# Root-mean-square means as two fp32r products, a reordered start-up, and reordered entries of two layers, in a fp32 network on one core

## What is computed

```python
def rmsnorm(x, g):
    xf = x.astype(jnp.float32)
    y = xf * lax.rsqrt(jnp.mean(xf * xf, axis=-1, keepdims=True) + EPS)
    return (y * g.astype(jnp.float32)).astype(x.dtype)

def swiglu(x, w_gate, w_up, w_down):
    return (jax.nn.silu(x @ w_gate) * (x @ w_up)) @ w_down

    h = x
    for l in range(DEPTH):                      # first_block
        h = h + 0.5 * swiglu(rmsnorm(h, ffn1_norm[l]), ffn1_w_gate[l], ffn1_w_up[l], ffn1_w_down[l])
        u = rmsnorm(h, mix_norm[l])
        z = u @ w_in[l]
        ...
        h = h + merged @ w_out[l]
        h = h + 0.5 * swiglu(rmsnorm(h, ffn2_norm[l]), ffn2_w_gate[l], ffn2_w_up[l], ffn2_w_down[l])
    return rmsnorm(h, final_norm)

        h = rms_norm(x, even_norm_g[i])         # second_block, layer 0
        proj = h @ even_w_in[i]
        ...
        x = x + jnp.concatenate([o_a, o_b], axis=-1) @ even_w_out[i]

        h = rms_norm(x, odd_norm_g[i])          # second_block, layer 1
        proj = h @ odd_w_in[i]
        q, k, v, z, r = jnp.split(
            proj, [GLA_KEY, 2 * GLA_KEY, 2 * GLA_KEY + GLA_VAL,
                   2 * GLA_KEY + 2 * GLA_VAL], axis=-1)
        log_a = jax.nn.log_sigmoid((r @ gla_w_gate[i] + gla_b_gate[i]).astype(jnp.float32)) / GLA_TAU
        ...
        x = x + (o * jax.nn.silu(z)) @ odd_w_out[i]
```

## Time and profile before

| | |
|---|---|
| time, median of 3 runs | 1449.96 us (1448.96 to 1450.06) |
| the profiled execution's own time | 1450.0 us |
| its span in the trace | 1448.1 us |
| granted TensorE clock | 1.00 of full speed |
| TensorE busy | 1441.7 us, 12390 matmul records |
| VectorE, ScalarE, GpSimd busy | 1051.4, 782.1, 99.2 us |
| moved by DMA | 261.37 MB, mean 180 GB/s |

### The profile page before, as it was taken

The page is one execution under the profiler, slowest core; times in us unless marked ns, Lnnn a source line. Parts: engine busy times, 40 slices in busy tenths (PEclk is TensorE's granted clock), DMA queues, the critical chain, the costliest instruction groups (busy, mean ns, idle before and its releaser), DMA issues.

```text
span 1448.1 us, 28457 instructions
## 1 busy us (share of the span) xinstructions
PE 1441.7 (100%) x12390; PEld 1392.2 (96%) x12390; DVE 1051.4 (73%) x1434; ACT 782.1 (54%) x1014; POOL 99.2 (7%) x77
## 2 busy tenths in 40 slices
PE   9999999999999999999999999999999999999999
PEld 8999998999999999999999899999999999989978
DVE  6766676797876655766558689888787799666844
ACT  6544556575554444544436566455645655775753
POOL 0000010210000000000001020000000037300000
PEclk9999999999999999999999999999999999999999
DMA  8655546444555655556554544466655454435531
GB/s 324 226 186 201 177 155 211 154 147 150 200 196 193 204 180 199 196 184 203 184 201 139 201 146 161 161 218 222 203 185 196 146 202 151 143 107 176 193 139 59
DMA packets 38844, 261.37 MB, mean 180 GB/s; under 512 B 4672, under 2 KB 5184, under 8 KB 9152
## 3 DMA queue, kind: packets, MB, share of 16 engines
q1 hardware_dynamic: 38576, 259.54, 52.2%
q10 hardware_dynamic: 144, 0.00, 0.0%
HBM read 258.48 MB, written 1.05 MB: 179 GB/s over the span
## 4 chain that ended last, share of the span: by engine, by line
PE 98%; DVE 1%; DMA 1%; ACT 0%; SPq 0%; issue 0%
PE ps L257 30%; PE ps L259 30%; PE ps L258 30%; PE ps L1549 1%; PE ps L1564 1%; DMA w_raw<-in_weights 1%; PE ps L1540 0%; PE ps L1522 0%; PE ps L2432 0%; DVE w_low L231 0%; PE ps L2866 0%; PE ps L2881 0%; PE ps L2453 0%; PE ps L2878 0%; PE ps L2465 0%; PE ps L1566 0%
## 5 line engine op out<-in xcount | busy, mean ns | idle before, releaser
L224 ACT ACTIVATE w_high<-w_raw 128x2048 fp32r<-128x2048 f32 (+1 forms) x243 | 457.3, 1883 | 478.9 <-PE ps L259 473.2
L231 DVE TENSOR_TENSOR w_low<-w_raw,w_high 128x2048 fp32r<-128x2048 f32 (+1 forms) x240 | 550.8, 2296 | 203.2 <-ACT w_high L224 202.9
L257 PE MATMUL ps<-x,w_high 128*128 128x256 f32 x2144 | 597.9, 279 | 1.4 <-DVE w_low L863 0.9
L259 PE MATMUL ps<-x,w_low 128*128 128x256 f32 x2144 | 593.2, 277 | 0.0
L258 PE MATMUL ps<-x,w_high 128*128 128x256 f32 x2144 | 593.1, 277 | 0.0
L257 PEld LDWEIGHTS ps<-x,w_high 128*128 128x128 f32 x2144 | 402.8, 188 | 6.3 <-issue 3.7
L258 PEld LDWEIGHTS ps<-x,w_high 128*128 128x128 f32 x2144 | 402.7, 188 | 0.7 <-issue 0.5
L259 PEld LDWEIGHTS ps<-x,w_low 128*128 128x128 f32 x2144 | 402.6, 188 | 0.0
L257 PE MATMUL ps<-ffn_hid,w_high 128*128 128x256 f32 x528 | 145.7, 276 | 0.0
L258 PE MATMUL ps<-ffn_hid,w_high 128*128 128x256 f32 x528 | 145.7, 276 | 0.0
L259 PE MATMUL ps<-ffn_hid,w_low 128*128 128x256 f32 x528 | 145.7, 276 | 0.0
(11 more groups left out here) (489 smaller groups left out, 2229.1 us busy)
## 6 DMA issues: line engine op xcount, KB each, us to landing
w_raw<-in_weights SPq DMA_DIRECT2D x229, 1024.0 KB, 4.9
w_raw<-in_weights SPq DMA_DIRECT2D x10, 768.0 KB, 4.3
setup_first<-in_first SPq DMA_DIRECT2D x8, 256.0 KB, 4.9
w_raw<-in_weights SPq DMA_DIRECT2D x4, 512.0 KB, 5.5
even_second_vectors<-in_second SPq DMA_DIRECT2D x1, 1836.0 KB, 7.8
w_raw<-in_weights SPq DMA_DIRECT2D x2, 640.0 KB, 4.0
resid<-in_x SPq DMA_DIRECT2D x1, 1024.0 KB, 9.8
out<-resid SPq DMA_DIRECT2D x3, 256.0 KB, 2.4
```

The costliest lines, as they stand in the source:

```text
L224: act.activation(self.slot(self.wh, n)[:, f], self.slot(self.raw, n)[:, f], ACT.Copy).then_inc(self.hi_made, 1)
L231: dve.tensor_tensor(self.slot(self.wl, n), self.slot(self.raw, n), self.slot(self.wh, n).bitcast(F32), ALU.subtract).then_inc(self.lo_made, 1)
L257: pe.matmul(out, ah, bh, start=start, stop=False, skip_group_check=True)
L259: return pe.matmul(out, al, bh, start=False, stop=stop, skip_group_check=True)
```

## The change

1. *Means.* The sum of squares is split like any operand (`Norm.part`: two more VectorE operations of 256 columns, into `sum_parts`), and the mean is two fp32r matmuls with a matrix `share` of 1/D in fp32r (`exact2`), in place of the fp32 matmul. 1/1024 is exact in fp32r. The share and the parts are 64 B apart modulo 512. Even's mean over `even_q` stays fp32.
2. *Addresses.* No FFN slot stands at the odd distance any more, but the table slots of the last FFN.
3. *Start-up.* The eight pieces now hold x, gate and up (384 KB each, the first in two transfers), and TensorE takes the two slots interleaved, piece by piece (`first_pair`). Slot 2 comes in two halves and is split in four parts, with the sums of the squares between them on VectorE. Slots 3 and 4 are loaded without waiting for a buffer. The warm-up has 11 matmuls and waits for less.
4. *Last FFN and Even.* VectorE makes a slot's low part before the second part of the next norm's sum. The fp32r mean comes behind slot 1, the fp32 one within slot 2, S5's first input products within slot 3, which goes to PSUM bank 5.
5. *Odd.* The slots are q, q, R, k, k, ...; the mean comes within slot 1, the gate product in the middle of slot 3.

```diff
-SLOT_PARTS = (PIECES, 4, 2)
-WARM = 9
+PAIR_PARTS, THIRD_PARTS = PIECES + 1, 4
+WARM = 11
...
-G_R, G_Q, G_K, G_V, G_Z, G_OUT, ODD_SLOTS = 1, (0, 2), 3, 5, 9, 13, 17
+G_R, G_Q, G_K, G_V, G_Z, G_OUT, ODD_SLOTS = 2, (0, 1), 3, 5, 9, 13, 17
...
-FIRST_AT, APART_AT, LAST_AT = ffn_at((3,)), ffn_at((2,)), ffn_at((2, *TABLE_SLOTS))
+FIRST_AT, APART_AT, LAST_AT = ffn_at(()), ffn_at(()), ffn_at(TABLE_SLOTS)
...
+            self.parts = inner.enter_context(nc.sbuf_tensor("sum_parts", [P, 2, SEQ], F32R))
...
+        self.share = sb("share", [P, P], F32R)
...
-        if n >= RING:
+        if n >= RING + 2:
...
+def exact2(pe, out, a, bh, bl):
+
+    pe.matmul(out, a, bh, start=True, stop=False, skip_group_check=True)
+    return pe.matmul(out, a, bl, start=False, stop=True, skip_group_check=True)
...
+def first_pair(c, pe, banks):
+
+
+    for k in range(DT):
         pe.wait_ge(c.xl_made, k + 1)
-    if k % (DT // parts) == 0:
-        pe.wait_ge(c.lo_made, sum(SLOT_PARTS[:n]) + k * parts // DT + 1)
+        for n, bank in enumerate(banks):
+            wh, wl = c.weights_at(n, DT, FC)
+            pe.wait_ge(c.lo_made, k + 2 if k else n + 1)
+            for i in range(2):
+                f = slice(i * P, (i + 1) * P)
+                mm = exact3(pe, c.halves(bank)[:, i, :], wh[:, k, f], wl[:, k, f], c.xh[:, k, :], c.xl[:, k, :],
+                            k == 0 and i == 0, k == DT - 1)
+            if k == DT - 1:
+                mm.then_inc(c.done, 1)
...
-        return dve.tensor_tensor(sq[:, 0, :], sq[:, 0, :], sq[:, 1, :], ALU.add)
+        return dve.tensor_tensor(sq[:, 2, :], sq[:, 0, :], sq[:, 1, :], ALU.add)
+
+    def part(self, dve):
+        c, whole = self.c, self.c.sq[:, 2, :]
+        c.dve_link(dve.tensor_scalar(c.parts[:, 0, :], whole, 1.0, None, ALU.mult))
+        dve.tensor_tensor(c.parts[:, 1, :], whole, c.parts[:, 0, :].bitcast(F32), ALU.subtract).then_inc(c.sum_made, 1)
 
     def add(self, dve):
         dve.wait_ge(*self.squared(4))
-        self.add_up(dve, self.c.sq).then_inc(self.c.sum_made, 1)
-
-    def average(self, pe, bank, sq):
-        return pe.matmul(self.c.bank(bank, SEQ), self.c.ones[:, 0, :], sq[:, 0, :], start=True, stop=True)
+        self.c.dve_link(self.add_up(dve, self.c.sq))
+        self.part(dve)
+
+    def average(self, pe):
+        c = self.c
+        pe.wait_ge(*self.summed(1))
+        return exact2(pe, c.bank(self.bank, SEQ), c.share[:, :], c.parts[:, 0, :], c.parts[:, 1, :])
 
     def mean(self, pe):
-        pe.wait_ge(*self.summed(1))
-        self.average(pe, self.bank, self.c.sq).then_inc(self.c.mean_made, 1)
+        self.average(pe).then_inc(self.c.mean_made, 1)
...
+    def add_early(self, dve):
+        c, sq = self.c, self.c.sq
+        dve.wait_ge(*self.squared(2))
+        dve.tensor_tensor(sq[:, 0:2, :], sq[:, 0:2, :], sq[:, 2:4, :], ALU.add)
+        dve.wait_ge(*self.squared(4))
+        c.dve_link(dve.tensor_tensor(sq[:, 4:6, :], sq[:, 4:6, :], sq[:, 6:8, :], ALU.add))
+
+    def add_halves(self, dve):
+        c, sq = self.c, self.c.sq
+        c.dve_link(dve.tensor_tensor(sq[:, 0:2, :], sq[:, 0:2, :], sq[:, 4:6, :], ALU.add))
+
     def add(self, dve):
-        sq = self.c.sq
-        dve.wait_ge(*self.squared(4))
-        dve.tensor_tensor(sq[:, 0:2, :], sq[:, 0:2, :], sq[:, 2:4, :], ALU.add)
-        dve.tensor_tensor(sq[:, 4:6, :], sq[:, 4:6, :], sq[:, 6:8, :], ALU.add).then_inc(self.c.sum_made, 1)
-
-    def average(self, pe, bank, sq):
-        for k in self.LEFT:
-            mm = pe.matmul(self.c.bank(bank, SEQ), self.c.ones[:, 0, :], sq[:, k, :], start=(k == 0), stop=(k == self.LEFT[-1]))
-        return mm
+        c, sq = self.c, self.c.sq
+        c.dve_link(dve.tensor_tensor(sq[:, 2, :], sq[:, 0, :], sq[:, 1, :], ALU.add))
+        self.part(dve)
+
+    def mean(self, pe):
+        pe.wait_ge(self.share_made, 1)
+        super().mean(pe)
...
+    def mean_first(self, pe):
+        self.average(pe).then_inc(self.e.first_mean, 1)
+
     def mean(self, pe):
-        pe.wait_ge(self.e.sum_made, 1)
-        self.average(pe, B_SUM + 1, self.e.sq).then_inc(self.c.mean_made, 1)
-        pe.wait_ge(*self.summed(1))
-        self.average(pe, B_SUM, self.c.sq).then_inc(self.e.first_mean, 1)
+        c, e = self.c, self.e
+        pe.wait_ge(e.sum_made, 1)
+        pe.matmul(c.bank(B_SUM + 1, SEQ), c.ones[:, 0, :], e.sq[:, 2, :], start=True, stop=True).then_inc(c.mean_made, 1)
...
         c.split_low(dve, base + down_at(LAST - 1) + RING)
         self.next.add(dve)
+        c.split_low(dve, base + down_at(LAST) + RING)
         self.next.add_more(dve)
-        c.split_low(dve, base + down_at(LAST) + RING)
...
+        sp.dma_start(self.room[:, 0, 0:2], self.first[:, 0, 0:2]).then_inc(self.piece_in[0], 16)
+        sp.dma_start(self.room[:, 0, 2:3], self.first[:, 0, 2:3]).then_inc(self.up_in, 16)
+        for b in range(1, PIECES):
             sp.dma_start(self.room[:, b], self.first[:, b]).then_inc(self.piece_in[b], 16)
-        for b, s in enumerate((self.half_in, c.landed[1])):
+        for b, s in enumerate((self.half_in, c.landed[2])):
             half = slice(b * SLOT // 2, (b + 1) * SLOT // 2)
-            sp.dma_start(c.slot(c.raw, 1)[:, half], c.weights[1][:, half]).then_inc(s, 16)
-        for n in range(2, EARLY_SLOTS):
+            sp.dma_start(c.slot(c.raw, 2)[:, half], c.weights[2][:, half]).then_inc(s, 16)
...
+            if b:
+                self.pair_high(act, b)
+                continue
+            self.pair_high(act, 0, slice(0, 1))
+            act.wait_ge(self.up_in, 16)
+            self.pair_high(act, 0, slice(1, 2))
...
+        self.norm.add_early(dve)
+        self.third_low(dve, 0)
+        self.norm.add_halves(dve)
+        self.third_low(dve, 1)
         self.norm.add(dve)
-        for b in range(SLOT_PARTS[2]):
-            self.low_part(dve, 2, b)
+        self.third_low(dve, 2)
+        self.third_low(dve, 3)
...
+def even_bank(u):
+    return 5 if u == A_IN_AMID else u % 3
...
+        after(0)
         self.norm.reciprocal(dve)
         for n in range(A_GLU):
...
+        amid = {2: {2: lambda: self.norm.mean(pe)}, A_IN_AMID: {DT // 2: lambda: s5_in(*A_IN[A_IN_AMID])}}
...
             if n == 1:
-                self.norm.mean(pe)
+                self.norm.mean_first(pe)
             if 0 <= n - A_SUFFIX < PAIRS:
                 suffixes(n - A_SUFFIX)
             if n in A_Y:
                 s5_out(A_Y.index(n))
-            if n in A_IN:
+            if n in A_IN and n != A_IN_AMID:
...
+        def gate_product():
+            pe.wait_ge(self.read_d, odd_emptied(G_R))
+            for h in range(H):
+                mm = pe.matmul(c.halves(3 + h // 2)[:, h % 2, :], E[:, O_WG + h * P:O_WG + (h + 1) * P], o.r[:, :],
+                               start=True, stop=True)
+            mm.then_inc(self.gate_sum, 1)
+
+        amid = {1: {2: lambda: self.norm.mean(pe)}, G_K: {DT // 2: gate_product}}
...
                 four_columns(pe, c.bank(b, SEQ), c.narrow[base + n][0], c.h).then_inc(c.done, 1)
-                self.norm.mean(pe)
...
-                project(c, pe, b, base + n, DT).then_inc(c.done, 1)
-            if n == 2:
-                pe.wait_ge(self.read_d, 2)
-                for h in range(H):
-                    mm = pe.matmul(c.halves(3 + h // 2)[:, h % 2, :], E[:, O_WG + h * P:O_WG + (h + 1) * P], o.r[:, :],
-                                   start=True, stop=True)
-                mm.then_inc(self.gate_sum, 1)
```

More of the change, by code:

```diff
@@ L754, in tensor @@
             mean = lambda: self.norm.mean(pe)
+            if s == 0 and base == 0:
+                first_pair(c, pe, (B_GATE, B_UP))
+                continue
             if s > 1:
@@ L847, in arrived, with third, pair, pair_high @@
     def arrived(self, b):
         return self.piece_in[b], 16 if b else 32
-    def part(self, t, n, b):
-        size = SLOT // SLOT_PARTS[n]
-        return self.c.slot(t, n)[:, b * size:(b + 1) * size]
-    def high_part(self, act, n, b):
+    def third(self, t, b):
+        size = SLOT // THIRD_PARTS
+        return self.c.slot(t, 2)[:, b * size:(b + 1) * size]
+    def pair(self, t, b, which):
+        return t[:, which, AT[0] + b * FC:AT[0] + (b + 1) * FC]
+    def pair_high(self, act, b, which=slice(0, 2)):
@@ L855, in high_part, with pair_low @@
         c = self.c
-        raw = self.part(c.raw, n, b) if n else self.weights[:, b, :]
-        act.activation(self.part(c.wh, n, b), raw, ACT.Copy).then_inc(c.hi_made, 1)
-    def low_part(self, dve, n, b):
+        act.activation(self.pair(c.wh, b, which), self.weights[:, b, which, :], ACT.Copy).then_inc(c.hi_made, 1)
+    def pair_low(self, dve, b, which=slice(0, 2)):
         c = self.c
-        raw = self.part(c.raw, n, b) if n else self.weights[:, b, :]
-        dve.wait_ge(c.hi_made, sum(SLOT_PARTS[:n]) + b + 1)
-        dve.tensor_tensor(self.part(c.wl, n, b), raw, self.part(c.wh, n, b).bitcast(F32), ALU.subtract).then_inc(c.lo_made, 1)
```

(26 more changed lines are left out.)

75 lines of the change are left out of this document (45 added, 30 removed).

## The result

The changed kernel takes 1455.32 us (median of 4, 1455.08 to 1455.69), the kernel before 1449.82 beside it. The ratio is 1.0039, with a 95% interval of 1.0027 to 1.0051: slower by 5.5 us, where 1447.1 was forecast. It is rival B that came, at 1453.7 in the forecast. The median is 1.4 us above my range, since other terms were off too.

A forecast was written before the change was run, and what follows sets the result against it. TensorE was taken as the bound (100% of the span), so only matmul count, spacing and waits count. Terms -1.47 - 0.4 - 2.0 - 0.15 + 1.1 = -2.9 from 1450.0 gave 1447.1 us; 8-in-10 range 1445.8 to 1453.9.

The forecast's parts named there:

- rival B: First FFN stays in the slow matmul spacing after the start-up's last wait, 6.4 to 6.8 us more: 1453.7 us; chance 0.22.
- case A: Whole kernel: the forecast as summed from its five terms, 1447.1 us, own range 1445.9 to 1448.7; chance 0.60.
- I give an entry behind a wait two chances in three of fast: Start-up: the odds that TensorE leaves its last wait before 35 us in the fast spacing, 113.3 ns a matmul.
- Term 1: Entries of three FFNs: with fp32r means 98 matmuls take 11.11 us instead of 11.60, saving 0.49 each, 1.47 us.
- Rival C: All four FFNs: the fp32r mean itself drops the fast spacing, 1475 us; chance 0.03.
- D: FFN entries: neither weight distance nor kind of mean sets the spacing, so the FFN means' saving goes, 1448.5 us; chance 0.08.
- Term 2: Two mixer entries: two fp32r matmuls take 0.227 us instead of 0.43 for the mean, saving 0.2 each, 0.4 us.
- Cover enough for 0.75: Mixer entries: slack between the sum's last addition and the mean hides VectorE's two more operations, 0.75 us together.
- Term 3: Start-up: pair ends at 17.9 us, slot 5 starts at 35.2 instead of 37.2; 2.0 us saved, bounds 1.4 and 2.3.
- Term 4: Last FFN and Even: slot 3 ends at 1177.15 us against 1177.3; 0.15 us saved, bounds -0.1 and 0.4.
- Term 5: Odd: new order brings TensorE waits of 0.75 and 0.95 us; 1.1 us lost in sum, bounds 0.2 and 1.5.
- The rule on SBUF ports: TensorE: read as making weight distance neutral, total 1448.5 us; the forecast set the trace's 118.1 against 113.3 ns against it.

## Why the prediction was wrong

- **The forecast's case.** I gave case A 0.60 and B 0.22. The step that failed is the chance of the spacing behind the last wait: "I give an entry behind a wait two chances in three of fast". In executions it is 1 of 13 for the changed kernel, 0 of 6 with the residual later. One wait alone isn't that bad: the pair's last wait was followed by the fast spacing in 5 of 12 traces, the one at slot 5 in 1 of 3. But I counted a single draw where there are two. A slow exit from the pair stays slow, since nothing is left to end it; a fast exit brings TensorE to slot 5 earlier, and there another wait can come. The mechanism, the place and the price of B were right: 6.30 us measured, just below the 6.4 to 6.8 forecast. That B and not A came was a matter of chance in each execution, only with far worse odds than I gave.
- **Why it is outside the range even so.** B's own figure, 1453.7, was 1.6 too low, and the range ended 0.2 above it. The mixers were 1.7 dearer than forecast, Odd 0.5, Even 0.2; the start-up and B's price were 0.3 cheaper each, and the kernel before took 0.2 less beside it. So the mixer term is what put the measurement outside.
- **What hung on it.** No slot at the odd distance was left to mend a slow exit, so every wait of the start-up had to end well. I saw that the slot in before ended the slow spacing, wrote that "the entry slots that go cost and save nothing beyond this if the mode is already fast", and didn't weigh the if.
- **Term 1, the FFN means.** 0.49, 0.49 and 0.50 measured, 0.49 each forecast; windows of 11.10 for 11.11. VectorE's two operations hid in the slack of the earlier trace rows. Rivals C and D fell: the fp32r mean keeps the fast spacing.
- **Term 2, the mixer means.** Forecast -0.2 each, measured +0.52 and +0.75. The step that failed is "Cover enough for 0.75". The sum itself had slack, but I asked only when the mean is used, not what is queued behind it on VectorE. In the kernel before, its operations run close on each other from 194 to 209 us with one gap of 0.39, ahead of rstd, and L1373 ended 0.2 us before TensorE needed it. The changed kernel's VectorE at this place:

```profile
199.30 0.72 DVE L397 TENSOR_SCALAR sum_parts<-scratch 128x256 fp32r<-128x256 f32 x1
200.06 0.43 DVE L398 TENSOR_TENSOR sum_parts<-scratch,sum_parts 128x256 fp32r<-128x256 f32 x1
200.40 2.29 DVE L236 TENSOR_TENSOR w_low<-w_raw,w_high 128x2048 fp32r<-128x2048 f32 x1
...
203.61 1.75 DVE L421 RECIPROCAL rstd<-rms 128x256 f32<-128x256 f32 x1
...
208.86 0.42 DVE L1437 TENSOR_TENSOR mix_arena<-mix_arena 128x256 f32<-128x256 f32 x1
```

  The two take 1.1 us from 199.30 to 200.40, not 0.75; they fill the gap ahead of rstd, and L1437 ends late for L1685. The mean's own saving came, 0.21; behind it 0.77 was lost (second mixer of this trace). The two runs with mixer means in fp32 confirm it: both are 0.00 there. Another 0.1 to 0.4 in a mixer lies further on, differs between traces, and stays open.
- **Term 3, the start-up.** -2.25 measured, -2.0 forecast, within its bounds. In part this was luck. The waits were 1.2 us, all in the pair, where 0.75 there and 0.25 in slot 2 were forecast, and the pair still ended at 17.9 because it ran fast from 10.27 on, which the forecast didn't have. The other trace of the same kernel, slow from the pair on, had -1.27, outside my bounds of 1.4 to 2.3.
- **Term 4, Even.** +0.09 measured, -0.15 forecast, inside its bounds. The wait for even_q's sum came with 0.5 (0.6 forecast).
- **Term 5, Odd.** +1.58 measured, +1.1 forecast, just above its bounds. Both waits came, 0.6 for odd_r and 1.0 for odd_k (0.75 and 0.95 forecast). By the starts +0.32 has come up to slot 4 (0.15 forecast) and +1.26 comes at the first V slots (0.95 forecast). What I had missed is that the fp32r mean has a price in the old order too: going back to that order gave 1.0 in the trace, and only the fp32 mean with it gave the rest.
- **Slips in the sums.** The bounds of the terms add up to 1445.6 to 1448.3 for A, not 1445.9 to 1448.7. Even's fp32 mean is priced at 0.24 in words, but two passes take 0.43, and the end of slot 3 fits 0.43. The wait in the first V slot is 0.95 in one place and 0.85 in another. Rival C's words add up to 1478; 1475 counts the 1.5 once. None of these decides anything.
- **The rule on SBUF ports.** By this case's runs the address of one slot changes a whole FFN by 5.7 us at a granted clock of 1.00. The Trainium skill, "TensorE: Matmul & The Clock Gate", section "Step-by-step: what each phase is for", says that TensorE has two independent SBUF read ports and that loading the next weights takes no bandwidth from the running matmul. That the distance is neutral was my reading of it; the runs contradict that reading, and the measurement decides. No run shows whether the ports have to do with it. Why two spacings exist, and what sets which one follows a wait, these runs don't show.

## What to carry to other kernels

Where a long stream of equal matmuls can run at two spacings, look in the trace for what ends the slow one, and keep one such step behind the last wait of each stretch. Here it cost 0.17 us where it wasn't needed and saved 5 to 6 where it was. Count the waits that must all end well, not only the last. Time such a kernel by its single executions and not by a median alone; a lone one 5 to 7 us off may be the other outcome. A single trace shows one outcome, and not how often it comes. And where an edit adds operations ahead of something with slack, follow the queue of that engine to its next gap: the slack of the step itself says nothing on those behind.
